# Value products and forget scores of the requests in four column quarters of 32 rows

## The reference, cut to what matters

```python
# forget (FoX) branch: 8 heads of 64, cached keys and values in 8 pages of 128 tokens
l = jnp.einsum('bthd,bshd->bhts', q, k) * scale
l = l + cq[..., None] - ck[:, :, None, :]          # decay of each head
o = jnp.einsum('bhts,bshd->bthd', masked_softmax(l), v)
# other (NSA) branches: 2 key-value heads with 4 query heads each
oc = jnp.einsum('bhgtn,bnhd->bthgd', pc, vc)       # 63 compressed blocks
osl = jnp.einsum('bhgtm,bhtmd->bthgd', ps, vg)     # selected blocks (here all 1024 cached tokens under a mask)
ow = jnp.einsum('bhgts,bshd->bthgd', pw, vw)       # window of 512
return g[..., 0:1] * oc + g[..., 1:2] * osl + g[..., 2:3] * ow
```

## Time and profile before

| | |
|---|---|
| median of 3 runs | 2427.85 us |
| span of the profiled execution | 2428.4 us |
| PE busy in it | 2369.9 us (98%) |
| VectorE, ScalarE, GpSimd busy | 1236.0, 547.6, 834.1 us |
| stage of the requests | about 746 to 999 us |

### The profile page before, as it was taken

The page is one execution under the profiler, slowest core; times in us unless marked ns, Lnnn a source line. Parts: engine busy times, 40 slices in busy tenths (PEclk is TensorE's granted clock), DMA queues, the critical chain, the costliest instruction groups (busy, mean ns, idle before and its releaser), DMA issues.

```text
span 2428.4 us, 30908 instructions
## 1 busy us (share of the span) xinstructions
PE 2369.9 (98%) x10983; PEld 1532.6 (63%) x10983; DVE 1236.0 (51%) x3115; ACT 547.6 (23%) x1328; POOL 834.1 (34%) x874
## 2 busy tenths in 40 slices
PE   8999999999998999999999999999999999999999
PEld 4544665555556777688886458888888874443343
DVE  4876716776773444522322794433334324229765
ACT  0001016666663333111111221111011110001131
POOL 0000004554454000475753453334333227203531
PEclk9999999999999999999999999999999999999999
DMA  5423830021018887632325301111111115543201
GB/s 185 106 82 86 273 113 20 1 81 59 1 57 226 234 232 199 209 87 78 87 73 156 83 31 53 36 36 53 35 46 42 36 48 202 175 143 135 84 18 57
DMA packets 185956, 240.28 MB, mean 99 GB/s; under 512 B 53436, under 2 KB 128834, under 8 KB 184266
## 3 DMA queue, kind: packets, MB, share of 16 engines
q1 hardware_dynamic: 181018, 218.99, 29.4%
q10 hardware_dynamic: 1168, 9.58, 1.3%
q0 software_dynamic: 3616, 9.73, 1.2%
HBM read 216.18 MB, written 37.99 MB: 105 GB/s over the span
## 4 chain that ended last, share of the span: by engine, by line
PE 56%; DVE 2%; ACT 1%; issue 0%; DVEq 0%; ACTq 0%
PE ps L2218 36%; PE ps L2382 11%; PE ps L2271 5%; PE ps L2439 2%; PE ps L2369 1%; DVE xT L153 1%; PE ps L2447 1%; ACT xT L2492 0%; PE ps L2275 0%; DVE arena L2970 0%; ACT arena L2589 0%; DVE stats L2644 0%; PE ps L2314 0%; DVE queries L2973 0%; DVE arena L1364 0%
## 5 line engine op out<-in xcount | busy, mean ns | idle before, releaser
L2218 PE MATMUL ps<-xT,arena 128*128 128x272 f32 x1920 | 472.7, 393 | 1.3 <-DVE arena L1375 1.3
L2218 PEld LDWEIGHTS ps<-xT,arena 128*128 128x128 f32 x1920 | 363.9, 190 | 77.0 <-DVE arena L1375 1.7
L2218 PE MATMUL ps<-queries,arena 128*128 128x272 f32 x1312 | 332.6, 393 | 1.8 <-DVE queries L2785 1.0
L2218 PEld LDWEIGHTS ps<-queries,arena 128*128 128x128 f32 x1312 | 249.6, 190 | 54.1 <-DVE queries L2785 1.4
L236 PE MATMUL ps<-arena,xT 128*128 128x512 f32 (+1 forms) x512 | 198.0, 549 | 2.1 <-DMA arena<-in_w_in 1.3
L1008 POOL TENSOR_SCALAR arena<-arena,gates 128x55 f32<-128x55 f32 (+15 forms) x192 | 123.2, 652 | 176.6 <-DVE arena L907 176.4
L943 ACT ACTIVATE arena<-arena 128x640 f32<-128x640 f32 (+15 forms) x256 | 164.7, 643 | 69.0 <-DVE arena L899 49.1
L236 PEld LDWEIGHTS ps<-arena,xT 128*128 128x128 f32 x512 | 97.7, 191 | 102.0 <-issue 93.0
L2218 PE MATMUL ps<-arena 128*128 128x272 f32 x576 | 148.6, 394 | 0.0
L798 PE MATMUL ps<-ident,arena 128*128 128x128 f32 (+4 forms) x880 | 137.8, 284 | 11.0 <-POOL arena L1008 5.2
L786 PE MATMUL ps<-arena,queries 64*128 64x512 f32 (+11 forms) x704 | 128.8, 465 | 14.2 <-DVE arena L899 11.4
(11 more groups left out here) (345 smaller groups left out, 3275.8 us busy)
## 6 DMA issues: line engine op xcount, KB each, us to landing
arena<-in_cache_fox_kv SPq DMA_DIRECT2D x72, 256.0 KB, 4.3
arena<-in_w_ffn_down SPq DMA_DIRECT2D x68, 256.0 KB, 3.3
arena<-in_w_in SPq DMA_DIRECT2D x16, 1024.0 KB, 5.3
xT<-in_w_ffn_down SPq DMA_DIRECT2D x64, 256.0 KB, 3.9
xT<-in_cache_fox_kv SPq DMA_DIRECT2D x56, 256.0 KB, 6.2
arena<-in_cache_nsa_kv SPq DMA_DIRECT2D x64, 192.0 KB, 7.8
arena<-in_w_ffn_up SPq DMA_DIRECT2D x11, 1024.0 KB, 5.4
arena<-in_w_ffn_gate SPq DMA_DIRECT2D x11, 1024.0 KB
```

The lines of the kernel that those rows point to most:

```text
L2218: mm = pe.matmul(ps[:, first + BANK_OF[z], 0:PIECE], weight[:, j, :], moving[:, j, :], start=(j == 0 and z in (1, 6, 5, 7)), stop=(j == kk ...
```

## The change

The partitions are put in another order: chunk c (two heads) x request r x head in chunk x token for the forget branch, so that each chunk has its own quarter of 32 partitions. The scores become eight matmuls of 32 weight columns per page, each quarter summed over the two requests (the queries of the other request are zeros). The forget values become four matmuls per page with 32 weight columns and 256 moving columns (the chunk's 128 channels of both requests); the new tokens' values become eight of 128 columns. The NSA values become four per tile, one per request and key-value head, with 64 columns. The outcome tiles shrink to 256 and 64 columns, and the decay rows come in four DMAs of 32 rows, permuted.

```diff
+def decay_rows(sp, at, io, n, there):
+    rows = io["neg_rows"][n * P:(n + 1) * P, :].rearrange("(r c x) k -> c r x k", r=2, c=4)
+    for c in range(4):
+        sp.dma_start(at.neg_c[32 * c:32 * (c + 1), :], rows[c]).then_inc(there, 16)
...
-        self.q_fox = at(2, 2, 320)
+        self.q_fox = at(2, 2, 4, 32)
...
-                for c in range(4):
-                    for r in range(2):
-                        mm = pe.matmul(ps[r * 64:(r + 1) * 64, F0 + p // 4, (p % 4) * P:(p % 4 + 1) * P],
-                                       at.q_fox[:, n % 2, r, c * 64:(c + 1) * 64], at.kT[:, p % 2, r, c, :],
-                                       start=(c == 0), stop=(c == 3))
+                for r in range(2):
+                    for c in range(4):
+                        mm = pe.matmul(ps[heads_of(c), F0 + p // 4, (p % 4) * P:(p % 4 + 1) * P],
+                                       at.q_fox[:, n % 2, r, c, :], at.kT[:, p % 2, r, c, :],
+                                       start=(r == 0), stop=(r == 1))
...
-                    for r in range(2):
-                        mm = pe.matmul(ps[r * 64:(r + 1) * 64, F0, :], at.pT_fox[:, j, r * 64:(r + 1) * 64], v[:, j % 4, r, :],
-                                       start=(j == 0), stop=False)
+                    for c in range(4):
+                        mm = pe.matmul(ps[heads_of(c), F0, 0:2 * P].rearrange("p (r d) -> p r d", r=2), at.pT_fox[:, j, heads_of(c)],
+                                       v[:, j % 4, :, c * P:(c + 1) * P], start=(j == 0), stop=False)
                     if j == NPAGE - 1:
                         for r in range(2):
-                            mm = pe.matmul(ps[r * 64:(r + 1) * 64, F0, :], at.pT_fox[0:64, 8, r * 64:(r + 1) * 64], keep.v_new[0:64, 0:FW],
-                                           start=False, stop=True)
+                            for c in range(4):
+                                mm = pe.matmul(ps[heads_of(c), F0, r * P:(r + 1) * P], at.pT_fox[0:64, 8, heads_of(c)],
+                                               keep.v_new[0:64, c * P:(c + 1) * P], start=False, stop=(r == 1))
...
-                for c in range(4):
-                    mm = turn(b, c * P, P, at.o_fox[:, c * P:(c + 1) * P])
+                for r in range(2):
+                    mm = turn(b, r * P, P, at.o_fox[:, r * P:(r + 1) * P])
...
                 for j in range(9):
-                    for r in range(2):
-                        kk = P if j < 8 else 64
-                        v = at.v_slc[:, r, j, :] if j < 8 else keep.v_new[0:64, FW:FW + P]
-                        mm = pe.matmul(ps[rows_of(r), S0, 2 * P:3 * P], at.pT_slc[0:kk, j, rows_of(r)], v, start=(j == 0), stop=(j == 8))
+                    for q in range(4):
+                        kk, d = P if j < 8 else 64, (q % 2) * HD
+                        v = at.v_slc[:, q // 2, j, d:d + HD] if j < 8 else keep.v_new[0:64, FW + d:FW + d + HD]
+                        mm = pe.matmul(ps[heads_of(q), S0, 2 * HD:3 * HD], at.pT_slc[0:kk, j, heads_of(q)], v, start=(j == 0), stop=(j == 8))
...
-                nc.vector.tensor_scalar(at.o_fox, ps[:, F0, :], fox_inv, None, ALU.mult).then_inc(o_saved, 1)
+                nc.vector.tensor_scalar(at.o_fox, ps[:, F0, 0:2 * P], fox_inv, None, ALU.mult).then_inc(o_saved, 1)
```

More of the change, by code:

```diff
@@ L755, in _ @@
                 sp.dma_start(ahead.block_no[half, :], io["c_block"]).then_inc(keep.const_in, 16)
-                sp.dma_start(ahead.fox_new[half, 56 + 8 * r:64 + 8 * r], io["c_newmask"]).then_inc(keep.filled_in, 16)
+                for c in range(4):
+                    sp.dma_start(ahead.fox_new[32 * c + 16 * r:32 * c + 16 * r + 16, 56 + 8 * r:64 + 8 * r], io["c_newmask"][0:16]).then_inc(keep.filled_in, 16)
             sp.wait_ge(win_copied, 16 * 26)
-            sp.dma_start(ahead.neg_c, io["neg_rows"][0:P, :]).then_inc(keep.neg_c_in, 16)
+            decay_rows(sp, ahead, io, 0, keep.neg_c_in)
             sp.wait_ge(logits_done, 2 * pair_no(1, LAST_TILE, CMP, 1) + 2)
@@ L1590, in fox_new_scores @@
                 b = enter(n, "fox_new")
-                for c in range(4):
-                    for r in range(2):
-                        mm = pe.matmul(ps[r * 64:(r + 1) * 64, b, 0:64], at.q_fox[:, n % 2, r, c * 64:(c + 1) * 64],
-                                       keep.newT[:, c, :], start=(c == 0), stop=(c == 3))
+                for r in range(2):
+                    for c in range(4):
+                        mm = pe.matmul(ps[heads_of(c), b, 0:64], at.q_fox[:, n % 2, r, c, :],
+                                       keep.newT[:, c, :], start=(r == 0), stop=(r == 1))
                 mm.then_inc(ring_filled, 1)
@@ L1719, in first_nsa_values @@
             def first_nsa_values(n):
-                for r in range(2):
-                    pe.matmul(ps[rows_of(r), S0, 0:P], at.pT_cmp[0:CMP_N, rows_of(r)], at.vc[0:CMP_N, r, :], start=True, stop=True)
+                for q in range(4):
+                    pe.matmul(ps[heads_of(q), S0, 0:HD], at.pT_cmp[0:CMP_N, heads_of(q)], at.vc[0:CMP_N, q // 2, (q % 2) * HD:(q % 2 + 1) * HD],
+                              start=True, stop=True)
                 for j in range(5):
-                    for r in range(2):
-                        kk = P if j < 4 else 64
-                        v = at.win[:, r, j, P:2 * P] if j < 4 else keep.v_new[0:64, FW + P:FW + 2 * P]
-                        pe.matmul(ps[rows_of(r), S0, P:2 * P], at.pT_win[0:kk, j, rows_of(r)], v, start=(j == 0), stop=(j == 4))
+                    for q in range(4):
+                        kk, d = P if j < 4 else 64, P + (q % 2) * HD
+                        v = at.win[:, q // 2, j, d:d + HD] if j < 4 else keep.v_new[0:64, FW + d:FW + d + HD]
+                        pe.matmul(ps[heads_of(q), S0, HD:2 * HD], at.pT_win[0:kk, j, heads_of(q)], v, start=(j == 0), stop=(j == 4))
             def last_nsa_values(n):
@@ L1922, in forget_turned @@
                         rows = slice(h * HD, (h + 1) * HD)
-                        columns = bank[rows, b * 512:b * 512 + 4 * 144].rearrange("p (c x) -> p c x", x=144)
+                        columns = ps[rows, b, r * P:(r + 1) * P].rearrange("p (c x) -> p c x", x=32)
                         ins = nc.vector.tensor_copy(keep.qfT[rows, :, T + 16 * n + 8 * r:T + 16 * n + 8 * r + 8],
-                                                    columns[:, :, r * 64 + 8 * h:r * 64 + 8 * h + 8])
+                                                    columns[:, :, r * 16 + 8 * h:r * 16 + 8 * h + 8])
                 ins.then_inc(ring_dve, 1)
```

31 lines of the change are left out of this document (17 added, 14 removed).

## The result

The changed kernel is slower: 2440.22 us (median of 4 runs, 2435.47 to 2442.58) against 2428.11 (2425.8 to 2431.33). The ratio is 1.0044 [1.003, 1.0058]. The forecast was 2410 us, with 0.82 for faster.

The account below looks back on a forecast made before the run. The PE was taken as the bound (busy 2369.9 of 2428.4 us), then late value pages; savings of 11.2 (pairs 0 to 2) + 6.6 (pair 3) + 0.3 (zeroing queries) = 18.1 gave 2410 us, 8-in-10 range 2395 to 2423.

Parts of the forecast that it names:

- two at a time: PE matmuls: bound where column quarters run only in twos, as halves do now, 0.43 to 0.44 ns per column.
- a full four: PE matmuls: bound where four column quarters run side by side, 0.21 ns per column of a record.
- the sum of 8.7 per pair: PE time saved per pair by scores, forget values, NSA values and outcome: 8.7 us, 35 over four pairs.
- Rivals 2, 3 and 4: PE: quarters run only two at a time, 2427 us (0.10); records supplied too slowly, moderate 2422 (0.10), strong 2448 (0.08).
- rival 4: PE: records supplied at only 85 ns each, NSA block 10.2 us instead of 4.0, total 2448 us; chance 0.08.
- the decay rows land 11.3 us after their issue, 35 us behind the 834.90: Decay-row transfers, timed from the next pair's keys leaving at 834.90: landing 5.9 us into the next pair, today 3.1.
- Key pages 4 to 7 queue behind the same rows: 1 to 1.5 us: Key page transfers behind the decay rows: 1 to 1.5 us, swallowed by the wait for page 7 except in pair 3.
- the shadow of page 7: PE's wait for the last value page, some 5 us per pair mostly for page 7, hiding earlier delays.
- What is late next: Value pages 4 to 7: PE waits some 5 us, so a period is 57.7 instead of 61.45, 3.75 saved of 8.7.
- Pair 0: 3.75 forecast: First pair, DMA share 0.98: same order of transfers, so the same 3.75 us saved as pairs 1 and 2.
- Pair 3: Last pair, no raw rows behind it: 6.6 us saved, from 3.5, 2.0, 0.5 and 0.6.
- Rival 1: Transfers of pages 4 to 7 come earlier with their release, so no gain is lost: 2393 us, periods near 53; chance 0.14.

Follow-up runs that it names:

- experiment 5: Next pair's key pages 0 to 3 issued behind value pages 4 to 7: 2417.82 us in the changed kernel with one decay DMA, 2428.5 in the kernel before.
- experiment 1: Changed kernel, decay DMAs of 32 neighbouring rows 2422.03 us, eight of 16 rows 2421.22, one of 128 2422.88; kernel before with the four decay DMAs 2449.96.
- experiment 2: Changed kernel with the outermost count of its four decay DMAs per pair at 4 instead of 2: 2426.72 us.

## Why the prediction was wrong, point by point

- **How fast a matmul runs: right.** Of the bounds "two at a time" and "a full four" I had chosen the second. The gains that the rows show: scores 0.45 per page (0.43 forecast), values 0.43 (0.43), NSA 1.5 (1.0, within the bounds). So the sum of 8.7 per pair was right or a little low, and one pair of one execution showed it whole (experiment 5). Rivals 2, 3 and 4 are refuted. Slower came, but not by rival 4's mechanism: the NSA block shrank.
- **The step that failed: "the decay rows land 11.3 us after their issue, 35 us behind the 834.90", and with it "Key pages 4 to 7 queue behind the same rows: 1 to 1.5 us".** I took the landing time of one DMA of 544 KB for four of 136 KB of another form, and of what is new in SP's list I priced only its 1.8 us of issue. The rows' bytes and number are the same, but the outermost count fell from 128 to 2. The last step of the decay rows came at 882.6, 20.2 us after the first of their issues, where I had 11.3. Key page 4 then came 5.1, 9.1 and 8.3 us late for the PE, and the clock fell behind it. Undoing that one step gives back 17 to 19 us (experiment 1), and the count between costs between (experiment 2). The last sentence of the prediction named a wait for decay rows "outside the shadow of page 7" at 1 us per pair: right in kind, seven times too small, and at the key pages.
- **What is late next: right in kind, too small in size.** Without the decay loss the PE does wait for value pages 4 to 7 (3.4 us in pair 1, 3.8 in pair 2), and page 7 lands 857.2 - 808.4 = 48.8 us after the start, where I had 50.2. Pair 1 takes 58.3 us, where I had 57.7; that this is so near is in part luck of the execution, for with DMAs of 32 neighbouring rows it took 62.6. Pairs 0 to 2 together are what repeats: 179 us in both, where I had 170.2, so nearly 9 us of the take-back were missing from my sum. One part that I left out is that the PE then runs at the 1.2 GHz level: pair 2 takes 60.2. In the kernel before, the clock was 1.00 in pairs 1 to 3, and I carried that over although I forecast the waits. With the clock kept up the two pairs take 56.2 and 57.1, so in this kernel the low clock accounts for the 3.1 us that were missing in them.
- **Pair 0: 3.75 forecast, mostly not there.** Its DMA share of 0.98 said that no slack was left; I had seen it, and gave it the gain all the same. With half the value bytes it takes 55.7; but it took 55.1 too in the kernel with DMAs of 32 neighbouring rows and all the bytes, so what holds pair 0 isn't shown. In the profiled execution of the kernel with one decay DMA, its 5.7 us, the 3.1 of pairs 1 and 2 and the later start of the stage (747.9 against 746.9) make up the 9.9 us between the 2410.3 of my sum and this kernel's profiled 2420.2.
- **Pair 3: right in its number.** 64.6 us in the kernel with one decay DMA instead of 71.3, 6.7 gained, 6.6 forecast (65.9 with DMAs of 32 neighbouring rows). Its clock was 0.94 and not the 1.00 that the sum took for granted, so part of the match is luck.
- **Rival 1, no take-back: refuted.** Page 7 lands 48.8 us after the start, where it was 51.1 (856.5 - 805.4) and the PE would have needed it by 45; the periods stay near 60 us, where the rival's sign was 53.

## What to carry to other kernels

A DMA whose rows are taken in another order is a new transfer, not the old one cut up: read its outermost count, and when it is small, price what queues behind it (here 0.5 MB per pair cost 17 to 19 us of 2440). Split it so that each piece has a larger outermost count (here 16, 32 and 128 all did). And when two transfers step one semaphore, their landing times are those of steps, not of transfers. And when work is taken from an engine that runs just ahead of its data, expect less than the work: here the PE then waited for transfers, and around the new waits the PE had stretches at half clock, of 3.5 us in one pair and 10 in the next.

## What the runs showed that I had not expected

- Four column quarters run nearly without loss: 64 records of 64 columns in 1.2 us (834.35 to 835.55), 19 ns each, where the shortest per record before was 35. The Trainium skill, TensorE: Matmul & The Clock Gate (Packing small matmuls, measured speedup), gives 2.38 times for three column tiles; by the rows of this case four tiles give 3.9.
- Late transfers with free engines: a key page takes 15 us, 28 of its 32 semaphore steps having come after 4, at a DMA share of 0.66.
- The clock: of two pairs with nearly the same four waits around the value pages (3.4 and 3.8 us in all), one had some 3.5 us at the 1.2 GHz level and the other 10 (912.6 to 922.9), the fall coming in the third wait. Useless matmuls ahead of these waits kept 1.00.
